# Starting a gemm pair before its root-mean-square norm is known, in a fused four-layer fp32 block

## The reference, cut to what matters

```
def rms_norm_2(x, gain):
    xf = x.astype(jnp.float32)
    y = xf * lax.rsqrt(jnp.mean(xf * xf, axis=-1, keepdims=True) + NORM_EPS)
    return (y * gain.astype(jnp.float32)).astype(x.dtype)

def hybrid_layer(x, ...):
    mod = jax.nn.silu(c) @ ada_w + ada_b
    sh_m, sc_m, gt_m, sh_f, sc_f, gt_f = jnp.split(mod[:, None, :], 6, axis=-1)
    h = rms_norm_2(x, norm_mix) * (1 + sc_m) + sh_m
    (aq, ak, av, bq, ...) = jnp.split(h @ w_in, points, axis=-1)
    ...                       # rope on aq, ak, bq; three kinds of attention, a delta rule
    x = x + gt_m * (jnp.concatenate([o_a, o_b, o_c], axis=-1) @ w_out)
    h = rms_norm_2(x, norm_ffn) * (1 + sc_f) + sh_f
    gate, up = jnp.split(h @ w_gate_up, 2, axis=-1)
    return x + gt_f * ((jax.nn.silu(gate) * up) @ w_down)
```

## Time and profile before

| what | value |
|---|---|
| runs | 2791.44, 2793.4, 2800.46 us (median 2793.4) |
| profiled execution | 2796.05 us, span 2794.6 us, mean granted TensorE clock 0.994 |
| TensorE busy | 2678.6 us (96% of the span) |
| VectorE busy | 1626.2 us (58%) |
| ScalarE busy | 1153.4 us (41%) |
| weight panel split, high (L2025) / low (L1276) | 404 times, mean 1051 / 1223 ns |

### The profile page before, as it was taken

One profiled execution on the slowest core, in us unless ns is written; L12 is line 12 of the kernel. 1 busy time (PEld: TensorE's weight loads), 2 busy tenths in 40 slices (PEclk: granted clock), 3 DMA queues, 4 the chain that ended last, 5 costly groups with the idle time before them and its releaser, 6 DMA issues.

```text
span 2794.6 us, 41766 instructions
## 1 busy us (share of the span) xinstructions
PE 2678.6 (96%) x17228; PEld 2115.5 (76%) x17228; DVE 1626.2 (58%) x2919; ACT 1153.4 (41%) x2012; POOL 9.4 (0%) x21
## 2 busy tenths in 40 slices
PE   7899999999999999999998899999999988999998
PEld 6677888867666788886886677888878766788886
DVE  7678646573556875667556765444465577533334
ACT  3544324234555442323645553221355466322222
POOL 0000000000000000000000000000000000000000
PEclk9999999999999999999999999999999999999999
DMA  8344555532221366563330013444443200322232
GB/s 311 105 152 166 195 173 181 181 126 99 76 70 60 112 205 195 189 197 121 106 122 16 3 61 121 143 144 146 138 136 107 87 3 2 98 91 98 98 99 83
DMA packets 92093, 336.42 MB, mean 120 GB/s; under 512 B 10480, under 2 KB 10736, under 8 KB 91776
## 3 DMA queue, kind: packets, MB, share of 16 engines
q1 hardware_dynamic: 86656, 314.87, 34.1%
q10 hardware_dynamic: 3936, 14.64, 1.5%
q0 software_dynamic: 1312, 4.23, 0.5%
HBM read 331.57 MB, written 2.13 MB: 119 GB/s over the span
## 4 chain that ended last, share of the span: by engine, by line
PE 46%; ACT 4%; DVE 3%; issue 1%; DVEq 0%; ACTq 0%
PE bank L659 12%; PE bank L660 12%; PE bank L661 12%; PE bank L938 1%; ACT probs L2272 1%; PE bank L923 1%; PE bank L909 1%; PE bank L1010 1%; PE bank L702 0%; PE bank L704 0%; PE bank L703 0%; PE bank L1172 0%; PE bank L1182 0%; PE bank L998 0%; PE bank L1120 0%
## 5 line engine op out<-in xcount | busy, mean ns | idle before, releaser
L1276 DVE TENSOR_TENSOR weights_low<-weight_ring,weights_high 128x1024 fp32r<-128x1024 f32 x404 | 493.7, 1223 | 424.4 <-ACT weights_high L2025 424.3
L659 PE MATMUL bank<-in_high,weights_high 128*128 128x512 f32 x1816 | 714.4, 393 | 16.7 <-DVE weights_low L1276 9.6
L660 PE MATMUL bank<-in_low,weights_high 128*128 128x512 f32 x1816 | 708.5, 390 | 0.0
L661 PE MATMUL bank<-in_high,weights_low 128*128 128x512 f32 x1816 | 708.4, 390 | 0.0
L2025 ACT ACTIVATE weights_high<-weight_ring 128x1024 fp32r<-128x1024 f32 x404 | 424.4, 1051 | 407.7 <-PE bank L661 301.1
L659 PEld LDWEIGHTS bank<-in_high,weights_high 128*128 128x128 f32 x1816 | 341.9, 188 | 96.4 <-issue 14.8
L661 PEld LDWEIGHTS bank<-in_high,weights_low 128*128 128x128 f32 x1816 | 342.0, 188 | 72.1
L660 PEld LDWEIGHTS bank<-in_low,weights_high 128*128 128x128 f32 x1816 | 342.2, 188 | 69.7 <-issue 0.2
L659 PE MATMUL bank<-hidden_split,weights_high 128*128 128x512 f32 x864 | 336.9, 390 | 0.0
L661 PE MATMUL bank<-hidden_split,weights_low 128*128 128x512 f32 x864 | 336.1, 389 | 0.0
L660 PE MATMUL bank<-hidden_split,weights_high 128*128 128x512 f32 x864 | 336.1, 389 | 0.0
(11 more groups left out here) (389 smaller groups left out, 3381.4 us busy)
## 6 DMA issues: line engine op xcount, KB each, us to landing
weight_ring<-stream SPq DMA_DIRECT2D x596, 512.0 KB, 3.5
mixer_out<-cmp ACTq DMA_DIRECT2D x6, 1024.0 KB, 4.9
hidden<-forget_rows POOLq DMA_DIRECT2D x16, 256.0 KB, 3.7
residual<-x ACTq DMA_DIRECT2D x4, 512.0 KB, 7.7
mixer_out<-cmp SPq DMA_DIRECT2D x2, 1024.0 KB, 6.2
out<-mixer_out ACTq DMA_DIRECT2D x4, 512.0 KB, 2.7
constants<-consts ACTq DMA_DIRECT2D x1, 1821.5 KB, 11.2
silu_c<-c ACTq DMA_DIRECT2D x2, 512.0 KB, 4.3
```

The source lines that it names most:

```text
L659: pe.matmul(bank[:, :], WHI[:, z, cols], high, start=(k == 0), stop=False)
L660: pe.matmul(bank[:, :], WHI[:, z, cols], low, start=False, stop=False)
L661: ins = pe.matmul(bank[:, :], WLO[:, z, cols], high, start=False, stop=(k == ktiles - 1))
L1276: v.tensor_tensor(WLO[:, z, :], ring[:, n % RING, :], WHI[:, z, :].bitcast(F32), ALU.subtract).then_inc(*mark("weights_low", "low", n))
```

## The change

At the three norm points the first two panels after the norm multiply the split of X*gain, without root and shift:

- New per output tile m before the norm point: ScalarE's `raw_high` (X*gain, rounded, into free slots of `hidden_split`), VectorE's `raw_low`. The low parts take the place of `mixer_out` (`raw_low` is an alias of it).
- New twice per norm point, after tiles 4 and 6, on VectorE: `raw_bias`, which multiplies a raw weight panel (in the ring) by the shift column and adds the eight blocks together in three further operations; TensorE sums the result over partitions with two one-column matmuls, ScalarE copies the two columns out of the bank.
- `square_sum` takes in tile 6 too, and for the last tile it stands ahead of `gated`; the mean has two matmuls (four passes) in place of three (six).
- TensorE: `raw_gemm` runs the pair at once, with the mean's and the shift's matmuls between its tiles, and without the five fillers. The next panel (gate 1, or ak) is the first to read the normalised tiles, and waits for them one by one.
- The pair's banks are evicted by VectorE with a multiplication by the root: the first inside `norm_split`, after the sixth H tile, the second behind it. The shift column is added by ScalarE in the silu (gate 0), by VectorE in a product (up 0), or by ScalarE in the rope's first copy (aq 0, aq 1), whose four swaps then read the sum from SBUF.
- The root lies in `probs_T` in place of `tmp`. SyncE's transfer of the first compression weights into `mixer_out` for layer 1 waits for the gemm of aq 1 in place of an event in layer 0.

```diff
+        def raw_gemm(event):
+            sums = before_raw(event)
+            def between(k):
+                if k == 1:
+                    pe.wait_ge(*at("partial", "ms", *sums))
+                    pe.matmul(B[3][:, :], const("mean"), H[:, 24, :], start=True, stop=False, skip_group_check=True)
+                elif k == 2:
+                    for i in range(2):
+                        pe.wait_ge(*at("raw_part", *event, i))
+                        ins = pe.matmul(B[2][:, i:i + 1], raw_part(i), ones[:, 0:1], start=True, stop=True)
+                    ins.then_inc(*mark("tensor_means", "raw_sum", *event))
+                elif k == 3:
+                    mean_of_rest(B[3], ("ms", *sums), (H[:, 31, :],), lambda j: ("x_square", *sums, j))
+            gemm_pair(raw_pair(event), raw_split, lambda k: ("raw_low", *event, k), between, idle=0)
...
-            mean_square(("hyb", l))
+            raw_gemm(("ffn", l))
...
+        def raw_low(event, m, gain):
+            v.wait_ge(*at("raw_high", *event, m))
+            v.scalar_tensor_tensor(RAWLO[:, m, :], X[:, m, :], gain[:, m:m + 1], raw_hi(m).bitcast(F32), ALU.mult,
+                                   ALU.subtract).then_inc(*mark("vector_norm", "raw_low", *event, m))
+        def raw_bias(event, i, shift):
+            sem, (n,) = "vector_raw", PANELS[raw_pair(event)[i]]
+            v.wait_ge(landed[n % RING], 16 * (n // RING + 1))
...
+            v.tensor_tensor(raw_prod, w, col, ALU.mult).then_inc(*step(sem))
+            for half in (4, 2):
+                v.wait_ge(*last(sem))
+                v.tensor_tensor(raw_prod[:, 0:half, :], raw_prod[:, 0:half, :], raw_prod[:, half:2 * half, :],
+                                ALU.add).then_inc(*step(sem))
+            v.wait_ge(*last(sem))
+            v.tensor_tensor(raw_part(i), raw_prod[:, 0, :], raw_prod[:, 1, :], ALU.add).then_inc(
+                *mark(sem, "raw_part", *event, i))
+        def raw_tiles(event, m, gain, shift):
+            raw_low(event, m, gain)
+            if m in (4, 6):
+                raw_bias(event, (m - 4) // 2, shift)
+        def raw_norm(event, gain, shift, outs):
...
+            def evict_raw(i):
+                v.wait_ge(*at("gemm", keys[i]))
+                v.tensor_tensor(outs[i], B_of(keys[i])[:, :], RAW_R, ALU.mult).then_inc(
+                    *mark("vector_raw", "evicted", keys[i]))
+            norm_split(event, lambda k: gain[:, k:k + 1], lambda k: shift[:, k:k + 1], RAW_R,
+                       between=lambda k: evict_raw(0) if k == 5 else None)
+            evict_raw(1)
...
             for m in range(KT):
+                if m == KT - 1:
+                    square_sum(("hyb", l), m - 1)
                 gated(("hyb_out", l, m), m, gate, ("x_new", "hyb", l, m))
-                square_sum(("hyb", l), m - 1)
+                if m < KT - 1:
+                    square_sum(("hyb", l), m - 1)
+                raw_tiles(("ffn", l), m, ffn_gain(l), hyb_mod(l, 3))
...
+            def rope_of_raw(key, scale):
+                s.wait_ge(*at("evicted", key))
+                s.activation(rope_raw(key), rope_rot(key), ACT.Identity, scale=scale, bias=raw_shift(key[2])).then_inc(
+                    *step("scalar_raw"))
...
-                sp.wait_ge(*(at("hyb_low", l - 1, 7) if l else at("ln_v", 3)))
+                sp.wait_ge(*(at("gemm", ("aq", l, 1)) if l else at("ln_v", 3)))
```

More of the change, by code:

```diff
@@ L373, in build @@
     M = sb("mixer_out", [P, KT, T])
+    RAWLO = sb_alias("raw_low", nc.sbuf_base, [P, KT, T], F32R)
     H = sb("hidden", [P, 32, T])
@@ L497, in build @@
     glast = COL[:, 32:64]
+    RAW = 6
+    raw_hi = lambda k: HSPLIT[:, 0, RAW + k, :]
+    raw_split = lambda k: (raw_hi(k), RAWLO[:, k, :])
+    raw_prod = H[:, RAW + KT:RAW + KT + 2, :].rearrange("p a t -> p (a t)").rearrange("p (k c) -> p k c", k=KT)
+    raw_part = lambda i: TMP[:, 1, i * P:i * P + P]
+    raw_shift = lambda i: COL[:, 120 + i:121 + i]
+    RAW_R = PT[:, 1, :]
+    raw_pair = lambda event: [("gate", event[1], 0), ("gup", event[1], 0)] if event[0] == "ffn" else ropes_of(event[1])[0:2]
+    is_raw = lambda event: event[0] == "ffn" or event == ("mix", 1)
+    before_raw = lambda event: ("hyb", event[1]) if event[0] == "ffn" else ("ffn", event[1] - 1)
     ulo = lambda n: U2[:, n, :]
@@ L749, in mean_of_sums, with mean_of_rest @@
             pe.matmul(bank[:, :], const("mean"), total, start=True, stop=False, skip_group_check=True)
-            for z in range(2):
-                pe.wait_ge(*at(*ready(KT - 2 + z)))
-                ins = pe.matmul(bank[:, :], const("mean"), tiles[z], start=False, stop=z == 1, skip_group_check=True)
-            ins.then_inc(*mark("tensor_means", *event, KT - 1))
+            mean_of_rest(bank, event, tiles, ready)
+        def mean_of_rest(bank, event, tiles, ready):
+            n = len(tiles)
+            for z in range(n):
+                pe.wait_ge(*at(*ready(KT - n + z)))
+                ins = pe.matmul(bank[:, :], const("mean"), tiles[z], start=False, stop=z == n - 1, skip_group_check=True)
+            ins.then_inc(*mark("tensor_means", *event, KT - 1))
+        def raw_gemm(event):
[12 more added lines that the diff above has]
+            gemm_pair(raw_pair(event), raw_split, lambda k: ("raw_low", *event, k), between, idle=0)
         def mean_step(bank, src, k, event):
@@ L989, in hybrid @@
         def hybrid(l):
[L990 removed]
+            ropes = ropes_of(l)
             def l2_sum(m):
@@ L1313, in conv4, with partial_sum @@
                 ins.then_inc(*(step(sem) if j < 3 else mark(sem, *event)))
-        def partial_sum(sem, total, tiles, m, event):
-            if 1 <= m <= KT - 3:
+        def partial_sum(sem, total, tiles, m, event, end=KT - 3):
+            if 1 <= m <= end:
                 if ev.value.get(sem):
@@ L1433, in norm_split @@
                     tile_low(k - 1)
+                between(k)
             tile_low(KT - 1)
@@ L1718, in hybrid @@
             v.wait_ge(*last("modulations"))
-            rms_norm(("mix", l), mix_gain(l), hyb_mod(l, 0))
+            if is_raw(("mix", l)):
+                raw_norm(("mix", l), mix_gain(l), hyb_mod(l, 0), [rope_rot(key) for key in ropes_of(l)[0:2]])
+            else:
+                rms_norm(("mix", l), mix_gain(l), hyb_mod(l, 0))
             def rope(key, dst):
@@ L1818, in hybrid @@
                     v.wait_ge(*last("residual"))
+                    if a + HALF >= FF2_T and m == KT - 1:
+                        square_sum(("ffn", l), m - 1)
                     gated(("fdown", l, a, m), m, gate, ("x_new", "ffn", l, a, m))
                     if a + HALF >= FF2_T:
-                        square_sum(("ffn", l), m - 1)
+                        if m < KT - 1:
+                            square_sum(("ffn", l), m - 1)
+                        if l + 1 < L2:
+                            raw_tiles(("mix", l + 1), m, mix_gain(l + 1), hyb_mod(l + 1, 0))
         def attention_and_delta(l):
@@ L2361, in hybrid @@
             s.wait_ge(*at("gains", l, 1))
-            rms_norm(("mix", l), ("in", 0) if l == 0 else ("ffn", l - 1), hyb_mod(l, 0))
+            if is_raw(("mix", l)):
+                raw_norm(("mix", l), hyb_mod(l, 0), 0.125)
+            else:
+                rms_norm(("mix", l), ("in", 0), hyb_mod(l, 0))
             def rope(key, scale, before):
@@ L2367, in rope @@
                 prepare(ahead(key))
+                if is_raw(("mix", l)) and key in ropes_of(l)[0:2]:
+                    rope_of_raw(key, scale)
+                    return
                 s.wait_ge(*at("gemm", key))
@@ L2375, in rope @@
                 ev.also("scalar_evict", "rope_in", key)
+            def rope_of_raw(key, scale):
+                s.wait_ge(*at("evicted", key))
+                s.activation(rope_raw(key), rope_rot(key), ACT.Identity, scale=scale, bias=raw_shift(key[2])).then_inc(
+                    *step("scalar_raw"))
+                s.wait_ge(*last("scalar_raw"))
+                for q in range(4):
+                    src = q ^ 1
+                    ins = s.activation(rope_rot(key)[32 * q:32 * q + 32, :], rope_raw(key)[32 * src:32 * src + 32, :], ACT.Copy,
+                                       scale=1.0 if q % 2 else -1.0)
+                    ins.then_inc(*(mark("scalar_raw", "rope_in", key) if q == 3 else step("scalar_raw")))
             def conv_in(m, before):
@@ L2504, in hybrid @@
                     if a + HALF >= FF2_T:
+                        if l + 1 < L2:
+                            s.wait_ge(*at("x_new", "ffn", l, a, m))
+                            raw_high(("mix", l + 1), m, mix_gain(l + 1))
                         squares(("ffn", l), ("ffn", l, a, m), m)
```

72 lines of the change are left out of this document (53 added, 19 removed).

## The result

The changed kernel takes 2808.9 us (median of 4 runs, 2808.6 to 2809.6) against 2792.4 us for the kernel before (4 runs, 2791.3 to 2800.5): a ratio of 1.0053, 95% interval 1.0034 to 1.0072. It is slower, and 8.8 us above the forecast of 2800.1 us. On a second chip it was 2808.3 us against 2794.8 (1.0047, 1.0035 to 1.0059).

What follows compares the result with a forecast made beforehand. TensorE, busy for 96% of the span, was taken as the bound, so only its gaps at the norm points could be saved. -0.6 + 5.8 + 1.5 = +6.7 us on 2796.05 gave 2802.8, in the median's terms 2800.1; range 2792 to 2807.

Steps and rivals of the forecast that it cites:

- the term for the clock: At "mix 1": the 7.4 us wait, now without fillers, is followed by a lower TensorE clock, +1.5 us.
- "ffn 0" and "ffn 1", -0.3 each: At both ffn norm points the 8.1 us loss is spent anew, so each saves only 0.3 us.
- S: Start of the first H tile, 1.53 us after the mean; forecast at E+8.7 for ffn, E+14.1 at "mix 1".
- The 24.48: At "ffn 0" before the change: us from the output projection's last matmul giving way (1680.42) to up 1's start (1704.90).
- my own walk: The forecast's step-by-step timing of TensorE, VectorE and ScalarE in instruction order around each norm point, counted from E.
- "mix 1", waits +5.8: At "mix 1" VectorE's backlog delays the pair and bq 0: a loss of 15.4 us against 9.6, +5.8.
- The 0.5 us for the landing of aq 0's panel: At "mix 1": the first `raw_bias` waits for aq 0's panel to land, adding 0.5 to the pair's start, E+7.4.
- Rival C: The clock falls at both "ffn" points too: +3.0 us, 2803.1; chance 20%.
- Rivals A and D: A: VectorE keeps up, -15.6 us, 2777.8, 7%. D: smaller or hidden VectorE backlog, clock holds, 2794.4, 20%.
- 2.65 us off: Correction from the profiled execution (2796.05 us) to the median of the runs, taking 2802.8 to 2800.1.
- my own sum: All three norm points and the clock: +6.7 us, 2802.8 profiled, 2800.1 in the median's terms; rival B, 53%.

Runs made afterwards that it cites:

- the late ones: Changed kernel with both products of weights and shift moved behind the last tile, their one-column matmuls to the pair's eighth step: 2803.0 us, 1.0034 of before.

## Why the prediction was wrong

In sign it was right (slower), and so were the waits; but it gave 0.58 to a time within 0.3% of before and 0.35 to the slower one that came, and the range (to 2807) ended 1.9 us below the time. The step that failed is the term for the clock.

E below is the end of the last projection's last matmul, as in the forecast: its start and 0.39 us.

- **"ffn 0" and "ffn 1", -0.3 each: right.** Forecast E+2.0 for the pair, E+8.7 for S, E+17.0 for gate 1, E+24.2 for up 1. With E at 1681.15 (1680.76 and 0.39) the changed kernel has:

```profile
1683.19 0.47 PE L716 MATMUL bank<-hidden_split,weights_high 128*128 128x512 f32 x1 [2.05 <-DVE residual L1376]
1698.04 0.50 PE L673 MATMUL bank<-in_high,weights_high 128*128 128x512 f32 x1 [1.47 <-DVE tmp L1495]
1705.12 0.47 PE L673 MATMUL bank<-in_high,weights_high 128*128 128x512 f32 x1 [1.31 <-DVE weights_low L1315]
```

  E+2.0, E+16.9, E+24.0, and S (1689.79) at E+8.6. The 24.48 for before mixed two views: 1704.90 is a time of the chain, in the timeline up 1 starts at 1704.74, which is E+24.3. Against that my own walk had saved 0.1 us a point, and 0.3 was measured.
- **"mix 1", waits +5.8: right within 0.5 us, but by luck, by two errors of opposite sign.** The 0.5 us for the landing of aq 0's panel was not there: VectorE starts the product right behind `raw_low`, and the pair started at E+6.8 (E at 2049.30) in place of E+7.4. On the other hand a backlog on VectorE does not start to cost at the norm point: `gated` 5 was late too, the last `fdown` panel needs its bank, and E itself came 1.2 us later (28.83 us behind the first `gated`, where it was 27.62): the wait of 0.9 us and the dearer first matmul behind it. 5.8-0.6+1.2 = 6.4; with fillers the stretch was 6.3 us longer than before.
- **The clock, +1.5: this is the step that failed.** It measured 4.9 us. I counted one fall, behind the longest wait, and priced it with what the earlier trace rows show of the stretch itself. The first fall alone cost 2.2 (the fillers gave that back up to bq 0; and S came 8.8 us behind the pair's start where the walk had 6.7). The second, behind the wait of 3.5 us at bq 0, I had not counted at all, although have a fall behind a wait of 2.7 and my own walk had a longer one there: 2.7 us. The rows of the changed kernel give nearly the same, as an estimate: in the stretches of 6.8 us at the lower level TensorE works for 4.6 and 5.6 us (from 2056.1 and from 2082.4 on), and half of that is 2.3 and 2.8.
- **Rival C** (falls at both "ffn" points, +3.0) happened at 5 of 16 points, at 1.7 us a fall, so +1.1 in the mean for the two. Rivals A and D did not happen: VectorE's idle share of 42% was no spare time where it was wanted.
- **The sum against the median.** 6.3+4.9-0.5 = 10.7 us on the profiled 2796.05 is 2806.8; the changed kernel's four profiled executions took 2807.1 to 2809.6. But I took 2.65 us off to go from that execution to the median of three runs; the longer series have the median at 2794.4 to 2796.8, that is at the profiled execution. Three runs 9 us apart don't place a median within 3 us. With that correction left out my own sum would have been 2802.8.

The Trainium skill, "TensorE: Matmul & The Clock Gate", Part 1, lets the clock follow recent activity. Four waits (7.6 and 2.7 us in the earlier trace rows, 6.8 and 3.5 here) agree, and so does the kernel with fillers; the length of the wait alone does not decide: behind 2.0 us at the "ffn" points the clock fell in 5 cases of 16, behind 3.7 us ahead of the pair it fell in the kernel without products and not in that with the late ones.

## What to carry to other kernels

Work moved off the path onto an engine with much idle time still queues there in order: ask what stands behind it in that queue, which bank or panel that frees, and whether the engine idles just before or just after. Here the products delayed the last eviction by 3.1 us, and the engine was idle for 5.3 us a moment later; but moved there, they delayed the norm by 1.3 us.

Price each new TensorE wait with the clock too, one by one, and not the longest alone: here waits of 6.8 and 3.5 us cost 4.9 us more at the lower clock. For shorter ones it is a chance and not a certainty (5 of 16 behind 2.0 us), so it belongs into the range. Where fillers are dropped with a change, count what they held up.

The same edit can gain at some sites and lose at another: here each site had its own spare time, and the edit at the two better ones, with its followers reordered, gave 0.9988 (by its interval only just under 1) where the whole gave 1.0047 to 1.0053.

## What the runs showed of the hardware that I had not expected

A product whose second operand repeats one column over 128 elements (L1473, 128x1024) took 1.22 us, no more than a plain subtraction of that size (L1315, 1.22 us).

The same code differs from one execution to the next by up to 3.9 us per attention stage, with the granted clock: 169.4 to 173.3 us over 18 profiled executions of all kernels, 169.6 to 173.2 within the kernel before. Two such stages account for up to 7.8 us of the spread of a kernel's runs (2790 to 2803 us for the kernel before).

Where TensorE is what all wait for, a fall cost half of the time that TensorE worked in it, here 2.2 and 2.7 us for stretches of 6.8 us. And the same wait of 3.7 us ahead of the pair was followed by a fall in one kernel and by none in another, so that two versions with nearly equal waits can differ by the clock alone.
